# Two modulation rows moved to other places of a two-block transformer kernel, with a root ahead of a copy and a product tile by tile

## What is computed

```python
def latent_attention(x, pos, w_in, q_a_gain, w_q_up, kv_a_gain, w_kv_up, q_gain, k_gain, w_out):
    h = x @ w_in                                    # 384 + 256 + 32 columns
    c_q, c_kv, k_rope = h[..., :B_Q_RANK], h[..., B_Q_RANK:B_Q_RANK + B_KV_RANK], h[..., B_Q_RANK + B_KV_RANK:]
    q = (rmsnorm(c_q, q_a_gain) @ w_q_up).reshape(B, S, B_HEADS, B_QK)
    kv = (rmsnorm(c_kv, kv_a_gain) @ w_kv_up).reshape(B, S, B_HEADS, B_NOPE + B_VDIM)
    ...                                             # norms, rope, causal softmax attention, @ w_out

def modulate(x, gain, shift, scale):
    return rms_norm(x, gain) * (1 + scale) + shift

def second_block(...):
    ...
    for i in range(DEPTH):
        m_lat = jnp.split((c_lat @ w_mod[i] + b_mod[i])[:, None, :], N_MOD, axis=-1)
        m_ctx = jnp.split(c_con @ w_mod[i] + b_mod[i], N_MOD, axis=-1)
        h_lat = modulate(x_lat, g_pre_mix[i], m_lat[0], m_lat[1])
        ...                                         # windowed attention (i = 0) or gated linear attention (i = 1)
        x_lat = x_lat + m_lat[2] * rms_norm(y_lat, g_post_mix[i])
        f_lat = channel_mlp(modulate(x_lat, g_pre_mlp[i], m_lat[3], m_lat[4]), w_mlp_in[i], w_mlp_out[i])
        x_lat = x_lat + m_lat[5] * rms_norm(f_lat, g_post_mlp[i])
```

## Time and profile before

| | us |
|---|---|
| median of 3 runs | 2412.01 |
| lowest, highest | 2402.62, 2412.06 |
| profiled execution | 2407.69 |
| its span in the trace | 2406.4 |

### The profile page before, as it was taken

The page is one execution under the profiler, slowest core; times in us unless marked ns, Lnnn a source line. Parts: engine busy times, 40 slices in busy tenths (PEclk is TensorE's granted clock), DMA queues, the critical chain, the costliest instruction groups (busy, mean ns, idle before and its releaser), DMA issues.

```text
span 2406.4 us, 37928 instructions
## 1 busy us (share of the span) xinstructions
PE 2270.7 (94%) x16759; PEld 2067.7 (86%) x16759; DVE 1207.4 (50%) x1439; ACT 978.5 (41%) x1177; POOL 495.6 (21%) x447
## 2 busy tenths in 40 slices
PE   6999899999999999899999989999999999888998
PEld 6999898879999999667999966788888897667997
DVE  5645566656555555356655445362223264545444
ACT  3433444444433443244435346443322334444442
POOL 2112343421211221121222111002211201221220
PEclk9999999999999999799999999999999999899999
DMA  7555443354555555598555311123323232113551
GB/s 248 172 174 166 142 140 123 128 205 154 179 176 193 176 173 189 195 311 297 182 176 175 114 36 36 36 95 100 103 92 100 96 127 88 36 53 122 176 188 58
DMA packets 205246, 344.73 MB, mean 143 GB/s; under 512 B 8845, under 2 KB 69498, under 8 KB 205082
## 3 DMA queue, kind: packets, MB, share of 16 engines
q1 hardware_dynamic: 205082, 342.31, 42.7%
HBM read 341.24 MB, written 1.05 MB: 142 GB/s over the span
## 4 chain that ended last, share of the span: by engine, by line
PE 80%; DVE 9%; POOL 5%; ACT 4%; issue 2%; SPq 0%; DMA 0%; DVEq 0%; POOLq 0%; ACTq 0%
PE PS L474 77%; PE PS L483 3%; DVE WL L460 3%; POOL small L1513 1%; ACT WH L444 1%; POOL small L1511 1%; POOL TMP L1522 1%; DVE XL L642 1%; DVE TMP L1439 1%; DVE small L1417 1%; POOL TMP L1523 0%; DVE TMP L1444 0%; DVE rstd L595 0%; DVE al L2632 0%; DVE al L1428 0%
## 5 line engine op out<-in xcount | busy, mean ns | idle before, releaser
L460 DVE TENSOR_TENSOR WL<-raw,WH 128x2048 fp32r<-128x2048 f32 (+2 forms) x281 | 651.6, 2331 | 684.4 <-ACT WH L444 684.4
L474 PE MATMUL PS<-XH,WH 128*128 128x256 f32 (+1 forms) x2368 | 699.4, 295 | 21.8 <-DVE WL L460 11.0
L474 PE MATMUL PS<-XL,WH 128*128 128x256 f32 (+1 forms) x2368 | 696.2, 294 | 0.0
L474 PE MATMUL PS<-XH,WL 128*128 128x256 f32 (+1 forms) x2368 | 696.1, 294 | 0.0
L444 ACT ACTIVATE WH<-raw 128x2048 fp32r<-128x2048 f32 (+2 forms) x281 | 519.0, 1858 | 362.0 <-PE PS L474 361.4
L474 PEld LDWEIGHTS PS<-XH,WH 128*128 128x128 f32 x2368 | 455.8, 192 | 34.9 <-DVE WL L460 12.2
L474 PEld LDWEIGHTS PS<-XL,WH 128*128 128x128 f32 x2368 | 455.9, 193 | 8.8
L474 PEld LDWEIGHTS PS<-XH,WL 128*128 128x128 f32 x2368 | 455.8, 192 | 8.8
L474 PE MATMUL PS<-WH,XH 128*128 128x256 f32 (+2 forms) x944 | 288.8, 306 | 18.3 <-DVE XL L642 8.5
L474 PE MATMUL PS<-WL,XH 128*128 128x256 f32 (+2 forms) x944 | 280.3, 297 | 0.0
L474 PE MATMUL PS<-WH,XL 128*128 128x256 f32 (+2 forms) x944 | 279.9, 296 | 0.0
(11 more groups left out here) (247 smaller groups left out, 2518.3 us busy)
## 6 DMA issues: line engine op xcount, KB each, us to landing
raw<-in_ffn_w_in SPq DMA_DIRECT2D x88, 1024.0 KB, 5.1
raw<-in_w_mod SPq DMA_DIRECT2D x48, 1024.0 KB, 5.3
raw<-in_ffn_w_out SPq DMA_DIRECT2D x40, 1024.0 KB, 4.9
raw<-in_a_w_in SPq DMA_DIRECT2D x36, 1024.0 KB, 4.9
raw<-in_w_mlp_in SPq DMA_DIRECT2D x32, 1024.0 KB, 5.4
raw<-in_w_mlp_out SPq DMA_DIRECT2D x32, 1024.0 KB, 4.9
raw<-in_gla_w_in SPq DMA_DIRECT2D x12, 1024.0 KB, 5.4
raw<-in_attn_w_qkv SPq DMA_DIRECT2D x6, 1024.0 KB, 5.1
```

Source lines behind the costliest of these rows:

```text
L460: dve.e.tensor_tensor(self.WL[j % NRAW][:, 0:nk * nn], self.raw[j % NRAW][:, 0:nk * nn], wh.bitcast(F32), ALU.subtract).then_inc(*self.lo. ...
L474: return self.pe.e.matmul(out, l, r, start=start, stop=stop, skip_group_check=skip)
```

## The change

Of the rows between the latent attention's input products and its transposes only one stays. One stands ahead of the first input product now, and one more in the linear attention's end, between the sums y1 and n1; the last turn, which stood there, comes behind the sums n1. Every row between these places has a number smaller by one than before. Since the rows' chunks stand ahead of `b_w_in` and of the last MLP's first chunks in the stream, `act_begin` and `dve_begin` would no longer reach these, and two pairs of calls of `act_part` and `dve_part` split them where they were split before. In the linear attention's end ACT's root comes between the square and the copy of y's second half. The last MLP's first product goes through all four blocks for each tile (`tiles=True`), and no longer through the tiles for each block.

```diff
-FILL_LATENTS = 3
+FILL_LATENTS = 1
...
-    def pe_linear(self, src, x, b0, T, name, tag="", mid=None):
+    def pe_linear(self, src, x, b0, T, name, tag="", mid=None, tiles=False):
...
-            for b in range(nb):
+            order = [(b, k) for k in range(nk) for b in range(nb)] if tiles else [(b, k) for b in range(nb) for k in range(nk)]
+            for b, k in order:
...
-                    m = self.mm3(out, (wh[:, k, o], wl[:, k, o]), (xh, xl), kt == 0, kt == nk_all - 1)
+                m = self.mm3(out, (wh[:, k, o], wl[:, k, o]), (xh, xl), kt == 0, kt == nk_all - 1, tiles)
...
             self.act_begin(6)
+            if s == 2 and half:
+                self.act_part()
+                self.act_part()
...
             self.dve_begin(6)
+            if s == 2 and half:
+                self.dve_part()
+                self.dve_part()
...
         QR = [four(self.TMP[:, 768 * w:768 * w + 768]) for w in range(2)]
+        self.pe_mods.send((2, 3))
...
+        self.fill_act(2)
+        self.act_settle()
...
+        self.dve_mods.send(3)
...
             if last:
                 act.e.activation(SQ, p, ACT.Square).then_inc(*self.sq_act.up(key))
+            if root:
+                root()
             act.e.activation(y, p, ACT.Copy).then_inc(*self.y_act.up(key))
...
         if nxt:
-            self.pe_mods.send((0, 2))
+            self.pe_mods.send((1, 5))
             for q in range(2):
                 self.pe_sums(t + "n1", 1, q, self.tiles(self.nSQ[1]), self.sq_act, (t + "n1", q), 4, False)
+            self.pe_mods.send((1, 5))
 
     def last_product_act(self, t, first, l, sub, n_chunks, nxt, free):
         for half in range(2):
             self.act_begin(n_chunks)
-            self.to_y_act((t, half, 1), half, 1, self.PS[:, 4 * half:4 * half + 4, 0:256], (t, "o", half), first, True, free)
-        self.act_root(t + "y1", 1, 0)
+            if nxt and half:
+                self.act_part()
+                self.act_part()
+            root = (lambda: self.act_root(t + "y1", 1, 0)) if half else None
+            self.to_y_act((t, half, 1), half, 1, self.PS[:, 4 * half:4 * half + 4, 0:256], (t, "o", half), first, True, free, root)
         if nxt:
+            self.fill_act(1)
+            self.act_settle()
             self.act.wait_ge(self.lin, (t, "o", 1))
             self.squares_act(t + "n1", 1, self.tiles(self.nSQ[1]), [[(self.res, (t, 1, q))] for q in range(2)])
             self.act_root(t + "n1", 1, 4)
-            self.fill_act(0)
-            self.act_settle()
...
         if nxt:
-            self.dve_mods.send(2)
+            self.dve_mods.send(5)
             self.dve_invert(t + "n1", 1)
             self.prenorm_dve(t + "n1", 1, *self.next_norm(l, sub), self.tiles(self.nXF[1]), [(self.lin, (t, "o", 1))])
+            self.dve_mods.send(5)
...
-                    self.pe_linear(w_in[:, c0:c0 + 512], xs, b0, T, name)
+                    self.pe_linear(w_in[:, c0:c0 + 512], xs, b0, T, name, tiles=l == 1 and grp + i == 0)
```

More of the change, by code:

```diff
@@ L511, in pe_linear @@
                     out = self.PS[:, b0 + b, :].rearrange("p (h t) -> p h t", h=2)
[L512 to L521 removed]
+                kt = k0 + k
+                xh, xl, ready = x(kt)
+                pe.wait_ge(self.lo, c)
+                for signal, key in ready:
+                    pe.wait_ge(signal, key)
+                if kt == 0:
+                    self.pe_bank(b0 + b)
+                o = slice(b * 128, b * 128 + 128)
+                m = self.mm3(out, (wh[:, k, o], wl[:, k, o]), (xh, xl), kt == 0, kt == nk_all - 1, tiles)
             m.then_inc(*self.lin.up(c))
@@ L1975, in y_made, with to_y_act @@
         return (self.y_act if first else self.y_dve), key
-    def to_y_act(self, key, half, h, p, lin, first, last, free=()):
+    def to_y_act(self, key, half, h, p, lin, first, last, free=(), root=None):
         act = self.act
```

9 lines of the change are left out of this document (removed).

## The result

| kernel | median, us | lowest to highest | executions | ratio to before, 95% interval |
|---|---|---|---|---|
| before, beside it | 2406.95 | 2402.62 to 2412.06 | 5 | |
| changed | 2393.78 | 2393.32 to 2395.03 | 5 | 0.9938 [0.9921, 0.9955] |

The changed kernel is 13.2 us (0.6%) faster. The forecast was 2401.9 against 2412.01, 10.1 us, and gave "within 0.5%" the larger chance; the direction was right, the size was short by 3.1 us, and the measured time lies 0.8 us above the lower end of the range. The profiled execution of the changed kernel took 2395.03 us (span 2393.7) against 2407.69 (2406.4): 12.7 us.

A forecast was written before the change was run, and what follows sets the result against it. TensorE was taken as the bound: its wait for XL, its own order ahead of the transposes, and a chain at the linear attention's end. 9.4 + 0.2 + 0.5 = 10.1 us, giving 2397.6, carried to median 2401.9; range 2393 to 2409.

The forecast's parts named there:

- What bounds the three places: TensorE waits 3.46 us for XL, delays the transposes 10.4 us by its own order, waits for a chain at linear attention's end.
- The row ahead of the first product: Latent attention's start: the 3.46 us gap covers the row; the half clock behind it disappears, gain 1.0 us, bounds 0 and 1.3.
- Two rows fewer ahead of the transposes: Latent attention: first up product starts at 993.2 instead of 1002.6, 9.4 us including 1.0 of clock; bounds 8.4 and 12.1.
- The new wait under the splits: Latent attention: two up-weight splits on VectorE now stand between the scaling and the copies, 2.7 us.
- The row at the linear attention's end: Its product fits TensorE's 5.76 us gap; costs 0 to 0.9 us if all at half speed; nothing taken.
- The root: Linear attention's end: with ScalarE's root ahead of y's copy only the sums bind, gain 0.15 to 0.2 us.
- The tiles: Next layer's first product: all four blocks on each tile, never waits, 0.5 us; up to 2.1 at full clock.
- the sum: Whole kernel: 10.1 us off the profiled 2407.69 gives 2397.6, carried over to the median as 2401.9.
- The chances: Whole kernel, against a 0.5% line: faster 0.43, same 0.55, slower 0.01 or 0.02.
- Half given back: Latent loop: if memory sets its pace, the early arrival is partly waited for, 6.1 us cost, 2408; chance 0.11.
- Slower: Latent input products: clock falls and stays down through 144 matmuls, 13.0 us lost, 4 us slower, 2416; chance 0.04.
- Clock up: Up product's start, sums and first MLP product run at full speed: 5 us more, 2397; chance 0.12.

The follow-up runs named there:

- experiment 2: The kernel before, with only one modulation row moved from the latent attention to the linear attention's end; median 2401.29 us, ratio 0.998.
- the four shifted kernels: The changed kernel with 1.2, 2.4, 3.6 or 4.8 us of extra matmuls in the fourth feed-forward layer; medians 2398.11, 2398.53, 2398.69, 2402.73 us.
- experiment 4: The changed kernel with the splits of the two up weights placed earlier, ahead of the sums' chain; median 2390.39 us, ratio 0.9939.
- 11: The changed kernel with ScalarE's root behind y's copy again, as before; median 2396.01 us, ratio 0.9954.
- 4.8 us of shift: The changed kernel with 40 extra matmuls, results overwritten, in the fourth feed-forward layer; median 2402.73 us.
- five shifts: Kernel before and changed kernel, each with 0, 1.2, 2.4, 3.6 and 4.8 us of added matmuls; differences 13.2, 5.8, 8.7, 11.2, 8.4 us.
- experiment 9: The changed kernel with 24 dense matmuls, results overwritten, in the 3.60 us wait ahead of the transposes; median 2396.72 us, ratio 0.9958.
- all twenty kernels: All kernels profiled in the study; their profiled executions differ by 2.8 us in arrival at 960 us.
- the early splits: The kernel of experiment 4, also with 1.2 and 2.4 us added: medians 2390.39, 2397.91, 2399.37 us; mean 2395.9 against the changed kernel's 2396.8.

## Why the prediction was right, and where it was wrong

- **What bounds the three places: right.** The gap for XL, the rows ahead of the transposes and the chain at the linear attention's end behave as read.
- **The row ahead of the first product: right.** No matmul behind it was late, the clock stayed at 1.00 in 963.7 to 967 (1.0 us forecast, though the prediction's own 969.34 - 968.1 is 1.2; 1.13 measured at the end of the first input product), and removing this row's move brings the 0.51 back (experiment 2).
- **Two rows fewer ahead of the transposes: right.** 9.4 us forecast for the whole latent stage, 9.99 measured, and 10.0 within 0.1 in three of the four shifted kernels (10.4 in the fourth). The new wait under the splits is there: VectorE's copy came 2.4 us behind the scaling (2.7 forecast). Its worth was overrated, and with it the upper bound of 12.1 us: taking the splits away gives 1.6 us (experiment 4). The difference between 9.4 and 9.9 at the start of the up product is the scaling, over at 986.85 in place of 987.0, and copies at 989.25 in place of 989.7.
- **The row at the linear attention's end: covered.** Nothing was lost in the changed kernel. Where the stretches at half clock fall otherwise (experiments 2 and 11, and 4.8 us of shift) the stage takes 2.0 to 2.2 us more. 1.0 to 1.2 of them lie ahead of the row and can't be its doing; 1.0 to 1.1 lie in the second sums behind it, where the bound was 0.9. Whether the row had a part in that wasn't separated.
- **The root: right**, 0.14 us (0.15 to 0.2 forecast): it starts 0.04 us behind the sums, where the earlier trace rows give 0.18. No drain shows behind the table load.
- **The tiles: mis-sized.** 0.24 us for 0.5 forecast, at the same clock; and nothing against before in this execution (7.82 against 7.81 us from the first to the 48th matmul), since the half clock lasted longer over the product (to 2192.6, 4.8 us behind its start; before, to 2206.2, 4.2 us).
- **The step that failed** is the one behind the sum: that the time of all unchanged code is kept and the 10.1 us can be taken off the profiled time (2397.6) and carried over to the median (2401.9). In its place the runs showed 2.6 us more gained in unchanged code, 4.97 of it in the linear attention, and a median of before 5.1 us below the one that the difference was carried to. The stages with edits sum to the forecast (10.1 forecast, 10.1 measured), in part by luck, since the latent stage gave 0.6 us more and the tiles 0.5 less; and the mean over five shifts, 9.5 us, is nearer to the forecast than the direct comparison. But against before's profiled execution the linear attention alone takes up to 7 us less for no edit of its own, the last sums up to 1.7 more, and the two stages between the latent and the linear attention up to 1.3 and 1.5 more, with the added work taken off. No term and no part of the range had that, though the rows of the linear attention with their low clocks could have been read, and the range of the three times before (9.4 us) asked for a reason.
- **The chances.** By this, before's profiled execution was one with a slow linear attention (158.7 us, the long end), so a gain was more probable than a loss once anything moved. Faster by over 0.5% should have had more than 0.43.
- **The rivals.** Half given back: no, the latent stage from its up product on kept its length (87.81 us, before 87.88). Slower: no, the clock didn't fall in the input products. Clock up: it asked for 5 us more; some 3 came, but not where it said: before the up product the clock stood at 0.51 as before, and in the first product of the next layer at 0.50.

```profile
984.20:992.70 8.50, 2.80 (x10) 1.60 (x11) 5.79 (x12) 3.10 (x5) 1.18 (x3) 0.51 0.73 273
...
2188.00:2192.40 4.40, 4.40 (x21) 4.40 (x22) 4.40 (x13) 3.15 (x6) 0.00 (x0) 0.50 0.00 0
```

What stays open: what sets the moment at which the clock falls. Time at half clock alone doesn't give the stage's time (experiment 9: 34.1 us at half, 155.7 us; before: 34.1 and 158.7), since it matters which work it covers. That the clock is the cause is shown for the piece of 2082 to 2106 and for the last sums, where the same rows take their longer or shorter time with it; for the smaller differences around the grid attention, and for the executions without a trace, it is only argued.

## What to carry to other kernels

Work that nothing needs yet belongs into the gap ahead of the stage, and the price of moving it is what it used to cover: look on the other engines (here at VectorE's splits) for what comes into the open, and subtract what would be waited for anyway (here 2.4 us came into the open, and 1.6 were lost). Where the span holds stages at changing clock, a gain at one place is read stage by stage, each from its own start, and a difference of a few us in the total is believed only when it survives a shift of the arrival; a few harmless matmuls far from the edit make that test. A lowest median is not a proof either, as the early splits show.

## What the hardware showed

- The clock stood at half for 13.65 us (2093.6 to 2107.2 of before) while TensorE was busy in all of them, and in the latent loop for 3.4 us, twice, in one execution and not in another, over the same dense code. Busy matmuls behind a fall did not always bring it back at once. The Trainium skill, "TensorE: Matmul & The Clock Gate", section "What's actually happening", says that how many matmuls run at the low clock after a start differs from run to run of one kernel, by the phase of the gate. The traces here agree: the first product is the same in all twenty kernels, and 13 to 28 of its matmuls start at half before the full clock comes (at 26.8 to 29.9 us). They go further: it differs in the middle of a kernel too, and is worth up to 7 us of a stage of 159.
- 1.2 us of added work didn't cost its 1.2 us (2403.95 against 2404.45 of before beside it), and the executions of one unchanged program spread over 14.6 us on one chip, the longer ones at the lower mean clock (0.968 to 0.970 for 0.973 to 0.977).
- 24 dense matmuls in a wait kept the full clock through it (1.00 in 982.4 to 985.5), and it fell all the same under the sparse transposes behind (0.51 in 989.25 to 996).
